# A two-layer hybrid encoder in fp32: layer 1's first three gate/up units multiply x before its norm is known

## The reference, cut to what matters

```python
# D_MODEL 1024, SEQ 512, DEPTH 2, D_FF 2816, all float32
for l in range(DEPTH):
    sh1, sc1, g1, sh2, sc2, g2 = split(silu(c) @ w_ada[l] + b_ada[l], 6)
    h = rms_norm(x, norm1_g[l]) * (1 + sc1) + sh1
    za, zb, zq, zk, zv = split(h @ w_in[l])
    mix = concat([conformer_conv(za), short_gated_conv(zb), diff_attention(zq, zk, zv)]) @ w_out[l]
    x = x + g1 * mix
    h = rms_norm(x, norm2_g[l]) * (1 + sc2) + sh2      # rms_norm: x * rsqrt(mean(x*x) + eps) * g
    g, u = split(h @ w_gate_up[l])
    x = x + g2 * ((silu(g) * u) @ w_down[l])
```

## Time and profile before

| | before |
|---|---|
| median of 3 runs | 1195.58 us (1195.54 to 1195.77) |
| the profiled execution | 1195.6 us |
| its span, first to last instruction | 1193.5 us |
| TensorE busy | 1180.9 us, 99% |
| VectorE busy | 706.1 us, 59% |
| ScalarE busy | 493.7 us, 41% |
| mean granted TensorE clock | 1.000 |

### The profile page before, as it was taken

One profiled execution on the slowest core, in us unless ns is written; L12 is line 12 of the kernel. 1 busy time (PEld: TensorE's weight loads), 2 busy tenths in 40 slices (PEclk: granted clock), 3 DMA queues, 4 the chain that ended last, 5 costly groups with the idle time before them and its releaser, 6 DMA issues.

```text
span 1193.5 us, 14448 instructions
## 1 busy us (share of the span) xinstructions
PE 1180.9 (99%) x5208; PEld 933.7 (78%) x5208; DVE 706.1 (59%) x1021; ACT 493.7 (41%) x742; POOL 118.2 (10%) x195
## 2 busy tenths in 40 slices
PE   9999999999999999999999999999999999999998
PEld 6787556878888888888888875678888888888887
DVE  7989898985555433466667988756533333332221
ACT  5546787452222223322243468864423222232220
POOL 2411222110102000211000112100000000000000
PEclk9999999999999999999999999999999999999999
DMA  8687346885655232777323754322323232323332
GB/s 310 241 239 180 71 101 199 306 274 195 196 190 176 88 105 88 296 247 244 129 70 107 175 125 107 71 68 92 106 90 104 90 104 88 105 89 105 106 105 88
DMA packets 48940, 175.18 MB, mean 147 GB/s; under 512 B 5697, under 2 KB 5825, under 8 KB 48898
## 3 DMA queue, kind: packets, MB, share of 16 engines
q1 hardware_dynamic: 30386, 107.13, 27.3%
q0 software_dynamic: 18512, 67.51, 20.1%
HBM read 172.52 MB, written 2.10 MB: 146 GB/s over the span
## 4 chain that ended last, share of the span: by engine, by line
PE 89%; DVE 5%; ACT 4%; issue 1%; DMA 1%; SPq 0%; ACTq 0%; DVEq 0%
PE ps L1489 22%; PE ps L1491 22%; PE ps L1490 22%; PE ps L1550 4%; PE ps L1551 4%; PE ps L1552 3%; PE ps L1519 3%; PE ps L1730 2%; PE ps L1523 1%; ACT prob L716 1%; PE ps L1535 1%; PE ps L1536 1%; PE ps L1540 1%; PE ps L1705 1%; DVE neg_max L1177 1%
## 5 line engine op out<-in xcount | busy, mean ns | idle before, releaser
L604 ACT ACTIVATE w_hi<-raw 128x1024 fp32r<-128x1024 f32 x196 | 207.6, 1060 | 551.8 <-PE ps L1491 481.9
L941 DVE TENSOR_TENSOR w_lo<-raw,w_hi 128x1024 fp32r<-128x1024 f32 x164 | 201.3, 1228 | 255.3 <-ACT w_hi L604 255.1
L1489 PE MATMUL ps<-h_hi,w_hi 128*128 128x512 f32 x848 | 335.2, 395 | 0.0
L1491 PE MATMUL ps<-h_lo,w_hi 128*128 128x512 f32 x848 | 330.3, 390 | 0.0
L1490 PE MATMUL ps<-h_hi,w_lo 128*128 128x512 f32 x848 | 330.3, 389 | 0.0
L1489 PEld LDWEIGHTS ps<-h_hi,w_hi 128*128 128x128 f32 x848 | 159.2, 188 | 48.7 <-issue 17.3
L1491 PEld LDWEIGHTS ps<-h_lo,w_hi 128*128 128x128 f32 x848 | 159.2, 188 | 33.7
L1490 PEld LDWEIGHTS ps<-h_hi,w_lo 128*128 128x128 f32 x848 | 159.3, 188 | 32.0 <-issue 0.5
L1489 PE MATMUL ps<-gu_hi,w_hi 128*128 128x512 f32 x352 | 136.9, 389 | 0.0
L1490 PE MATMUL ps<-gu_hi,w_lo 128*128 128x512 f32 x352 | 136.9, 389 | 0.0
L1491 PE MATMUL ps<-gu_lo,w_hi 128*128 128x512 f32 x352 | 136.9, 389 | 0.0
(11 more groups left out here) (191 smaller groups left out, 1350.5 us busy)
## 6 DMA issues: line engine op xcount, KB each, us to landing
raw<-w_stream SPq DMA_DIRECT2D x196, 512.0 KB, 3.3
w_lo<-w_stream POOLq DMA_DIRECT2D x32, 512.0 KB, 8.0
ada_ring_gu<-ada POOLq DMA_DIRECT2D x28, 512.0 KB, 4.1
ada_ring_late<-ada POOLq DMA_DIRECT2D x28, 512.0 KB, 4.8
ada_ring_first<-ada POOLq DMA_DIRECT2D x16, 512.0 KB, 5.1
ada_ring_mid_a<-ada POOLq DMA_DIRECT2D x12, 512.0 KB, 5.3
ada_ring_mid_b<-ada POOLq DMA_DIRECT2D x12, 512.0 KB, 5.2
xT<-x_t SPq DMA_DIRECT2D x4, 512.0 KB, 5.7
```

Of the source, the lines that this page charges most:

```text
L604: act.activation(w_hi[:, u % RING, :], raw[:, u % RAW, :], ACT.Copy).then_inc(s_whi, 1)
L941: dve.tensor_tensor(w_lo[:, u % RING, :], raw[:, u % RAW, :], w_hi[:, u % RING, :].bitcast(F32), ALU.subtract).then_inc(s_wlo, 1)
L1489: pe.matmul(dst, whi, rhs[0][:, n, :], start=start, stop=False)
L1491: return pe.matmul(dst, whi, rhs[1][:, n, :], start=False, stop=stop)
```

## The change

In layer 1 the first three gate/up units (`N_LATE`) multiply x times the norm's gain, split into `xg_hi` and `xg_lo`, instead of h. The factor `rstd` of each token, and the product of the weights with the shift, join when the units are done. The shift's part is made by VectorE (`late_shift`: weights times shift, summed over the eight chunks) and by three small matmuls with ones. In layer 1 the halves at the last chunk and the unread matmuls fall away. In both layers the negation of a weight unit in the attention stage, and the DMA behind it, come a tile later than its high half (`NEG_AT`), and the taps are 4, 3, 3, 3, 0, 3, 3, 3, ..., 3 at tile 12, and in layer 1 3 at tile 0 and 0 at tile 4.

```diff
-TAPS_TILE = ((3, 3, 3, 3, 1, 3, 3, 4, 3, 2, 1, 3, 2, 0, 0, 0), (2, 2, 2, 2, 1, 2, 2, 2, 2, 1, 0, 2, 1, 0, 0, 0))
+TAPS_TILE = ((4, 3, 3, 3, 0, 3, 3, 3, 3, 2, 1, 3, 3, 0, 0, 0), (3, 2, 2, 2, 0, 2, 2, 2, 2, 1, 0, 2, 1, 0, 0, 0))
 STEP_AT = {1: 0, 3: 1, 6: 2, 9: 3, 11: 4}
+NEG_AT = {2: 0, 4: 1, 7: 2, 10: 3, 11: 4}
...
+            def x_gain_hi(k):
+                act.wait_ge(s_xnew, KC * (2 * L - 2) + k + 1)
+                act.activation(xg_hi[:, k, :], xT[:, k, :], ACT.Copy,
+                               scale=gain[:, L - 1, 1, k:k + 1]).then_inc(s_xghi, 1)
...
                 for s in range(N_OUT):
                     if s < N_OUT - 1:
                         step(U + U_OUT + s)
+                    if s < N_OUT - 1 or late:
                         square_x(2 * l + 1, s)
+                    if late:
+                        x_gain_hi(s)
...
+            def late_shift(j):
...
+                dve.tensor_tensor(late_w[:].rearrange("p (b c) -> p b c", b=KC),
+                                  raw[:, u % RAW, :].rearrange("p (b c) -> p b c", b=KC), shift,
+                                  ALU.mult).then_inc(s_lprod, 1)
+                dve.wait_ge(s_lprod, j + 1)
+                dve.tensor_reduce(late_sum[:, j, :], late_w[:].rearrange("p (b c) -> p c b", b=KC), AX_X,
+                                  ALU.add).then_inc(s_lsum, 1)
...
                     add_to_x(l, s, B_OUT[s], G1, U + U_OUT + s + 1)
+                    if l:
+                        norm_sum(2 * l + 1, s)
+                        x_gain_lo(s)
+                        if RING <= s < RING + N_LATE:
+                            late_shift(s - RING)
+                        if s < N_OUT - 1:
+                            split_lo(U + U_OUT + s + RING)
+                        continue
...
+            def late_stat(n):
+                pe.wait_ge(s_sum, (KC - 1) * (n - 1) + KC)
+                pe.matmul(ps[:, B_STAT, :], ones[:], sq_sum[:], start=True, stop=True).then_inc(s_nstat, 1)
+                for j in range(N_LATE):
+                    pe.wait_ge(s_lsum, j + 1)
+                    pe.matmul(ps[:, B_LATE, j * P:(j + 1) * P], late_sum[:, j, :], ones[:], start=True,
+                              stop=True).then_inc(s_lps, 1)
...
+                    late = [U + U_GU + j for j in range(N_LATE)]
+                    pe.wait_ge(s_xnew, 2 * KC * l + RING)
+                    units_by_chunk(late, range(N_LATE), order, s_xghi, s_xglo, 0, range(0, 1), (xg_hi, xg_lo))
+                    late_stat(2 * l + 1)
+                    units_by_chunk(late, range(N_LATE), order, s_xghi, s_xglo, 0, range(1, KC), (xg_hi, xg_lo))
+                    units_by_chunk([U + U_GU + N_LATE], [N_LATE], order, s_hhi, s_h, KC * (2 * l + 1))
```

More of the change, by code:

```diff
@@ L51 @@
 U_DOWN = U_GU + N_GU
+N_LATE = 3
 UNITS = U_DOWN + N_DOWN
@@ L300, in encoder_kernel @@
         B_HALF_STAT = (7, 4)
+        B_LATE = 5
         B_MIX = (7, 7, 7, 7, 3, 7)
@@ L868, in _ @@
                     if it in STEP_AT:
-                        step(U + U_B + STEP_AT[it])
+                        step(U + U_B + STEP_AT[it], neg=False)
+                    if it in NEG_AT and lo_by_dma(U + U_B + NEG_AT[it] + RING):
+                        split_neg(U + U_B + NEG_AT[it] + RING)
                     if it in (8, 12):
@@ L893, in _ @@
                 y_hi(l, 5)
+                late = l == L - 1
+                if late:
+                    act.wait_ge(s_gain, 2 * l + 1)
                 for s in range(N_OUT):
@@ L910, in _ @@
                 act.preload_act_table_set("silu_and_others")
-                with act.Fori(0, N_GU // 4) as i:
+                if late:
+                    for j in range(4):
+                        step(U + U_GU + j)
+                        f = j // 2
+                        if j % 2 == 0:
+                            act.wait_ge(s_lb, 1)
+                            act.wait_ge(s_late, j + 1)
+                            act.activation(wa[:, f, :], wa[:, f, :], ACT.Silu,
+                                           bias=late_bias[:, j:j + 1]).then_inc(s_sg, 1)
+                        else:
+                            act.wait_ge(s_pr, FC * l + f + 1)
+                            act.activation(gu_hi[:, f, :], wb[:, f, :], ACT.Copy).then_inc(s_ghi, 1)
+                with act.Fori(1 if late else 0, N_GU // 4) as i:
                     for j in range(4):
@@ L1037, in apply_halves, with x_gain_lo, norm @@
                                              ALU.mult).then_inc(s_t if half else s_thalf, 1)
-            def norm(l, which, u=None):
+            def x_gain_lo(k):
+                dve.wait_ge(s_xghi, k + 1)
+                dve.scalar_tensor_tensor(xg_lo[:, k, :], xT[:, k, :], gain[:, L - 1, 1, k:k + 1],
+                                         xg_hi[:, k, :].bitcast(F32), ALU.mult, ALU.subtract).then_inc(s_xglo, 1)
+            def late_shift(j):
+                u = UNITS * (L - 1) + U_GU + j
+                a = mod_at(SH2, 0)
+                shift = mod[:, L - 1, a:a + KC].unsqueeze(2).broadcast_to([P, KC, P])
+                dve.wait_ge(s_whi, u + 1)
+                if j:
+                    dve.wait_ge(s_lsum, j)
+                dve.tensor_tensor(late_w[:].rearrange("p (b c) -> p b c", b=KC),
[4 more added lines that the diff above has]
+                                  ALU.add).then_inc(s_lsum, 1)
+            def norm(l, which, u=None, halves=True):
                 dve.wait_ge(s_gain, 2 * l + which)
+                if not halves:
+                    dve.wait_ge(s_nrs, 2 * l + which + 1)
                 for k in range(KC + 1):
-                    if k == 0:
+                    if k == 0 and halves:
                         apply_halves(l, which)
@@ L1401, in _ @@
                         make_gain(0, 1)
-                    if s == N_OUT - 1:
+                    if s == N_OUT - 1 and not l:
                         add_halves(l, B_OUT[s], G1, U + U_OUT + s + 1)
@@ L1420, in _ @@
                     dve.wait_ge(s_mod, M_GU - M_MID)
-                norm(l, 1)
-                split_lo(U + U_GU + RING - 1)
+                if l == 0:
+                    norm(l, 1)
+                    split_lo(U + U_GU + RING - 1)
+                else:
+                    norm(l, 1, U + U_GU + RING - 1, halves=False)
                 def swiglu_step(i, first, first_mod=None):
@@ L1440, in swiglu_step, with late_ends @@
                                               gu_hi[:, 2 * i + f, :].bitcast(F32), ALU.subtract).then_inc(s_gu, 1)
+                def late_ends():
+                    dve.wait_ge(s_h, KC * (2 * l + 2))
+                    for j, dst in enumerate((wa[:, 0, :], wb[:, 0, :], wa[:, 1, :])):
+                        dve.wait_ge(s_unit, U + U_GU + j + 1)
+                        dve.tensor_tensor(dst, ps[:, j, :], rstd[:, 0, :], ALU.mult).then_inc(s_late, 1)
+                    split_lo(U + U_GU + RING)
+                    for j in range(4):
+                        f = j // 2
+                        if j % 2:
+                            dve.wait_ge(s_sg, FC * l + f + 1)
+                        if j == 1:
+                            dve.wait_ge(s_lb, 1)
+                            dve.wait_ge(s_late, 2)
+                            dve.scalar_tensor_tensor(wb[:, f, :], wb[:, f, :], late_bias[:, 1:2], wa[:, f, :], ALU.add,
+                                                     ALU.mult).then_inc(s_pr, 1)
+                        elif j == 3:
+                            dve.wait_ge(s_unit, U + U_GU + j + 1)
+                            dve.tensor_tensor(wb[:, f, :], ps[:, j, :], wa[:, f, :], ALU.mult).then_inc(s_pr, 1)
+                        if j:
+                            split_lo(U + U_GU + j + RING)
+                        if j % 2:
+                            dve.wait_ge(s_ghi, FC * l + f + 1)
+                            dve.tensor_tensor(gu_lo[:, f, :], wb[:, f, :], gu_hi[:, f, :].bitcast(F32),
+                                              ALU.subtract).then_inc(s_gu, 1)
                 begin = 1
@@ L1447, in _ @@
                 else:
-                    swiglu_step(0, True)
+                    late_ends()
                 with dve.Fori(begin, N_GU // 4) as i:
@@ L1507, in unit, with units_by_chunk @@
                 mm.then_inc(s_unit, 1)
-            def units_by_chunk(us, banks, order, hi_sem, lo_sem, base, part=range(KC)):
+            def units_by_chunk(us, banks, order, hi_sem, lo_sem, base, part=range(KC), rhs=(h_hi, h_lo)):
                 for u in us:
@@ L1788, in _ @@
                     unit(U + U_OUT + s, B_OUT[s], h, order)
[L1789 to L1793, removed]
+                if l == 0:
+                    norm_stat(2 * l + 1)
+                    units_by_chunk([U + U_GU, U + U_GU + 1], (0, 1), order, s_hhi, s_h, KC * (2 * l + 1))
+                    unit(U + U_GU + 2, 2, h, order)
+                    unit(U + U_GU + 3, 3, h, order)
+                else:
```

(2 more changed lines are left out.)

48 lines of the change are left out of this document (35 added, 13 removed).

## The result

| | before | changed |
|---|---|---|
| median | 1195.69 us (1195.54 to 1196.39, 6 runs) | 1202.26 us (1201.55 to 1202.93, 6 runs) |
| the profiled execution | 1195.6 us, span 1193.5 | 1202.93 us, span 1201.1 |

The account below looks back on a forecast made before the run. TensorE, busy 1180.9 of 1193.5 us, was taken as the bound. 1195.6 + 4.0 (unit 4 later) + 2.0 (clock) - 1.2 (attention) = 1200.4 us; range 1196.6 to 1203.0, the forecast's own 1199.0 to 1201.5.

Parts of the forecast that it names:

- the chance of 0.50: The forecast itself: TensorE waits some 7.4 us before the first xg matmul and the clock falls; 1200.4 us.
- the third rival: Late units on VectorE: shift product or reduction runs at half speed over spaced or broadcast views, three times 1.2 more; 1204.0 us, chance 0.12.
- The chances for slower: Whole kernel: chance that the change measures slower, above 1198.0 us, given as 0.72.
- two thirds of 0.18: Share of the first rival counted as slower: the clock stays up behind TensorE's wait, 1198.4 us, chance 0.18.
- TensorE stands still for the split of gate/up unit 2: Behind layer 1's output projection: TensorE waits some 7.4 us; VectorE's steps take 3.9 us, with the shift's part 6.3.
- The reduction, 1.14 of a step: VectorE's steps 4 to 6: summing the shift product over eight chunks takes some 1.2 us, with the overlap 1.14.
- The clock, 2.0 between 0 and 3.6: Behind TensorE's wait: the clock falls to 1.2 GHz and chunk 0 costs 2.0 us more; bounds nothing and 3.6.
- Unit 4 four us later, six with the clock: Layer 1's second norm: unit 4 starts 4.0 us later than at 852.82; the clock adds 2.0.
- What lies beside it costs nothing: Units 3 and 4: chunks of h, products with rstd and unit 4's split stay covered, by 2.2 us for the split.
- Attention, -1.2: Both layers' attention: without the negation in front, VectorE's mix comes 0.6 us earlier in each; -1.2, bounds 0 and -2.5.
- One sign: Attention: a sign of being right was that TensorE's waits for the mix come to about 1.3 us in all.
- Rival 4, the faster case: Output projection: VectorE doesn't lose the squares' time, TensorE waits 1.3 us, unit 4 starts 2.0 earlier; 1192.4 us, chance 0.07.

Follow-up runs that it names:

- the comparison within the stretch: The changed kernel with 36 unread matmuls in the wait before the first xg matmul, set beside the changed kernel from there to the small matmuls' end; 1200.79 us.
- Attention alone: The kernel before with only the attention part (negations and their DMAs a tile later, the taps moved): 1194.63 us, ratio 0.9989.
- the reordered kernel: The changed kernel with product and split over the square's wait in every step, reductions later, small matmuls behind chunk 7: 1191.02 us, ratio 0.9961.

## Why the prediction was right

Forecast were 1200.4 us and a range of 1196.6 to 1203.0; it came to 1202.26. That is in the range, but above the 1199.0 to 1201.5 given for the forecast itself. The mechanism was the one given the chance of 0.50, with one piece of the third rival. Two terms were too small, the reduction and the clock, and no error of the other sign hid them. (The chances for slower add up to 0.74, not 0.72: 0.50, two thirds of 0.18, and 0.12. The 14.99 in the price of an F32 matmul is the start of the instruction behind the earlier trace rows.)

*TensorE stands still for the split of gate/up unit 2*: right, and shown: with the shift left out the wait is 0.3 us, with the split ahead in four steps 6.6. Predicted were 7.4 us from the end of the last matmul, measured 9.5. The steps without the shift's part were right: s = 1 took 3.86 (801.11 to 804.97), and all four 15.9, as forecast. Those with it were 7.06, 6.95 and 6.89 instead of 6.25.

*The reduction, 1.14 of a step*: this is the mis-sized term. It took 2.00, 1.92 and 1.87 us. I had taken the contiguous row and put the price of a spaced view into rival 3; the reductions did what that rival says (1.6 times as long), the broadcast product did not (1.22). Three times 0.7 is the 2.1 us by which the wait was longer. The Trainium skill has the rule (Advanced Engine Details and Errata, "SBUF Cachelines": accesses that each fall on another 16-byte line pay a penalty), and both views, 512 B and 32 B apart, agree with it (1.87 to 2.13 us against 1.22). That section of the Trainium skill gives no figure, but it spoke against taking the contiguous row.

*The clock, 2.0 between 0 and 3.6*: the fall came, and cost 1.9 on chunk 0 (3.98 us for nine matmuls instead of 2.04) and 0.8 on the statistics (1.70 instead of 0.86), 2.8 by the comparison within the stretch. I had put the statistics into the bound of 3.6 and left them out of the 2.0.

*Unit 4 four us later, six with the clock*: it starts at 860.39 instead of 852.82, and the stretch began 1.2 us earlier (first add at 797.03 instead of 798.23), so the stretch grew by 8.8. That is 4.0 + 2.0 + 2.1 for the reductions + 0.8 for the clock, 8.9. With the 1.2 of attention it is the 7.6 us by which the span grew.

*What lies beside it costs nothing*: right. In the changed kernel no wait stands at unit 3, nor at unit 4, whose weights VectorE splits by 857.8, 2.6 us ahead.

*Attention, -1.2*: right in size. The first add of the output projection comes 1.20 us earlier, 0.67 of it from layer 0, and alone the part measures 1.2. The tap added to layer 1's tile 0 was priced at 0.65 and costs 0.7. One sign failed: the waits for the mix were to come to 1.3 us, and went from 2.5 to 2.1 only. Attention alone shows where part of the rest is: from the first mix of each layer to its first add, TensorE's busy time falls from 92.9 to 92.5 and from 86.8 to 86.6 us at the same number of instructions, so some of the gain was in pauses through which it counts as busy.

*Rival 4, the faster case*, had the right gain in it: 5.4 us of norm to be filled, of which the reordered kernel fills 3.3. It gets there with the same arithmetic, by the order of VectorE's steps and the place of the small matmuls.

## What to carry to other kernels

When work is pulled ahead of a wait, add up the engine that must prepare it over the whole window in which it is pulled: here VectorE had 27.6 us (797.03 to 824.64, the end of the output projection) and its chain took 36.9 (to 833.91). So the norm's 5.4 us, which the change was to fill, grew by 8.8, and 4.9 of those came through the clock (2.8) and the spaced reads (2.1). Order matters as much as amount: a step that adds, then waits for another engine's answer, should have its independent work between the two. And what isn't due for 15 us, as the shift's sum, belongs behind what is.

## What was not expected of the hardware

- VectorE's time for 1024 fp32 elements per partition goes from 1.22 us to between 1.87 and 2.13 when one view of the instruction, read 512 B or written 32 B apart, isn't contiguous. A broadcast operand costs nothing: the product with the shift takes 1.22, as the split does.
- Without unread matmuls TensorE stood still for 2.54 us at each of three norms, behind a few short matmuls of statistics, and the granted clock fell to half at each, at two of them only after TensorE had started again. Ten runs of that kernel spread over 1196.8 to 1201.9 us, where the kernel with ten unread matmuls in each norm stayed within 1195.55 to 1196.25.
